# Stacked low-rank decay products, and the gates' 24 columns as four column groups in single precision

## The chip, the cores and the metric

The kernel runs on one core of a Trainium2 chip. The metric is device microseconds of one execution. TensorE is called PE here; VectorE, ScalarE, GpSimd and SyncE are DVE, ACT, POOL and SP in rows of the profile. SP does no arithmetic here: it issues transfers, in order.

## What is computed

One layer of a streaming encoder on 1152 rows of 1024 values: a prompt of 1024 frames and eight running streams of 16 frames. The part that the change touches, cut from the reference:

```python
h = _rmsnorm(x, norm1)
gq, gk, gv, gr, glr, mq, mk, mv, mo, mi, mf = _split_proj(h @ w_in)
log_a = log_sigmoid(glr @ w_gla_a + b_gla_a) / 16     # glr: 16 columns; w_gla_a: 16 x 256
i_pre = mi + b_m_i                                    # 4 columns
log_f = log_sigmoid(mf + b_m_f)                       # 4 columns
# GLA:   S_new = exp(b_last) * S + k_dec^T v,  o = (q * exp(b)) S + scores v,   S = 0 for the prompt
# mLSTM: C_new = decay * C + (ws k)^T v,       num = qk v + w_inter * (q C),    C = 0 for the prompt
x = x + concat(o_A, o_B) @ w_out
x = x + conv_ffn(_rmsnorm(x, norm2))
```

So the projection has 24 narrow columns (mf, mi, glr: "the gates"), and the decay product multiplies the 16 low-rank columns by a 16 x 256 matrix.

## The kernel before

All large products are made in fp32r with both operands split into a high and a low half: `mm3` (lines 93 to 95) issues high x high, high x low and low x high into one accumulation. A weight piece is 128 x 1024; SP loads it into one of two `raw` slots, ACT copies it (high half, line 821), POOL subtracts (low half, line 749). Pieces live in six units in the order `W_ORDER`.

The work of the front part is one list, `front_order`, that every engine walks in this order, each doing its own share of an item, with semaphores between the engines. Rows are in three row blocks (rb) of 384. Items:
- `("turn", rb, half)`: PE transposes the scaled rows (line 957), ACT copies to the high half (837), DVE makes the low half (1160). Blocks 1 and 2 are turned in halves of four.
- `("gate", 0, rb)`: one unit of 24 products, 128 weight columns (24 of them used: mf at 0, mi at 32, glr at 64). DVE takes it from its bank by three or four instructions (lines 1170 to 1174), the low-rank rows into `glr`.
- `("t", t, rb)`: a unit of 24 products for tile t of gq, gk, mq, mk; DVE copies it out (1363), SP stores it.
- `("z", j, rb)`: decay product, 16 x 128 weights by 16 x 384, in single precision (1120); DVE adds the bias (1367).
- `("logs",)`: log-sigmoid of the decays and of the forget gate. DVE line 1179 and 1181, then ACT three Exp (904) and three Ln (908).
- `("n", g, r)`: 128 rows of gv, gr, mo or mv, 24 products of 512 columns; k runs over four weight pieces, two k for each.
- `("w", i)`: ACT and POOL split piece i. From piece 6 on the rule below puts it ahead of the unit after the last use of the piece six earlier, and on ACT it stands at that place of the list, behind whatever is listed ahead of it:

```python
where[i] = min(max(n if shared else n + 1, where[i - 2] + 3, where[i - 1]), len(units))
```

PSUM banks of the front form a ring of four; a unit waits until the entry four before it has been taken. PE does the wait for a unit's weights (`piece_split`) and, for a tile, for all low halves of its row block (`lo_done`).

With that, the order of the kernel before is: gate 0, t0, t1 of block 0; half a turn; t2; half a turn; t3, gate 1; half a turn; t0 of block 1; half a turn; t1 to t3 of block 1; gate 2; t0 of block 2; six z; logs; t1 to t3 of block 2; nine rows of gv (g = 0, weight pieces 5 to 8); and so on with gr, mo, mv and the recurrence of the GLA in blocks of 128 frames (`outputs`, lines 1079 to 1103).

The back part walks `back_order` in the same way: products with w_out (`a` for the GLA half, `b` for the mLSTM half), transposes (`turn_a`, `turn_b` line 1818, `turn_n` line 1826) and the mLSTM (`numbers`, lines 1782 to 1789, `updates`, line 1806). Step 0 is the sample streams, whose states `C_s` SP loads at line 1539; steps 1 to 8 are the prompt. ACT line 1690 is `scaled`, which scales a row of x for `turn_n` when POOL's root (1625) is there. After it the feed-forward part runs to the end; it isn't touched.

Of the kernel before, what the change touches and what calls it, by code (L numbers as in the profile page):

```python
# [12 lines left out]
P = 128  # L13
# [188 lines left out]
def front_memory(nc):  # L202
    return Memory(nc, "p", [
        ("arena", [P, ARENA], F32), ("masks", [P, N_MASKS], F32), ("sig", [P, 512], F32), ("n_out", [P, 2, 512], F32),
        ("w_decay", [RANK, 2 * P], F32), ("gap", [P, 472], F32), ("t_out", [P, 4, RBW], F32), ("ss", [P, RT], F32), ("rstd", [P, RT], F32),
        ("rstd_h", [P, RT, H], F32), ("h1T_hi", [P, KD, ROWS], F32R), ("h1T_lo", [P, KD, ROWS], F32R)])
# [32 lines left out]
def scaled_memory(nc):  # L239
    return Memory(nc, "n", [("gap", [P, 19968], F32), ("rows", [P, JR, D], F32)])  # L240

# [43 lines left out]
def build(nc, a, o):  # L285
    with ExitStack() as top:
# [11 lines left out]
        mem_p, mem_m, mem_f, mem_n = front_memory(nc), back_memory(nc), ffn_memory(nc), scaled_memory(nc)  # L298
# [4 lines left out]
        done = front(nc, a, o, mem_p, mem_m, early, const, cols, col_m, col_d, ssq, power, w, raw, pb, bank, sem, block)  # L303
# [33 lines left out]
W_ORDER = ([PC_GATE] + [PC_T + t for t in range(4)] + [PC_N + 4 * g + q for g in (0, 2, 3, 1) for q in range(4)]  # L337
# [8 lines left out]
def front_order():  # L346
# [50 lines left out]
def pieces_of(x):  # L397
    if x[0] == "gate":
        return [0]
# [34 lines left out]
def front_entries(order):  # L434
    second = False
    out = []
    for x in order:
        second = second or x[:2] == ("n", 1)
        if x[0] in ("gate", "z", "cols", "flip"):
# [13 lines left out]
def front(nc, a, o, mem, mem_m, early, const, cols, col_m, col_d, ssq, power, w, raw, pb, bank, sem, block):  # L453
# [9 lines left out]
    wa = mem["w_decay"]  # L463
    ss, rstd, rstd_h = mem["ss"], mem["rstd"], mem["rstd_h"]

    def carve(at, *shapes):
        for shape in shapes:
# [4 lines left out]
            if len(shape) > 2:  # L472
# [9 lines left out]
    gu, z = (gu0, gu1, gu2), (z0, z1)  # L482
    ones_row, dg = gu0[0:H, 0:P], gu1[0:H, 0:(NC + NB) * H]
    m_ext, lf_ext, g_f, keep, glr = carve(RT * D, [H, EXT], [H, EXT], [H, ROWS], [H, ROWS], [RANK, ROWS])
# [19 lines left out]
             "level_step og_scaled root_step head_roots scored kdn_ready o_squared")  # L504
# [26 lines left out]
    def wait_taken(eng, name):  # L531
        owner, n = ring.taken(name)
        eng.wait_ge(taken[owner], n)

# [72 lines left out]
    def _(sp):  # L607
# [25 lines left out]
        sp.dma_start(const[:, :], a["ident"]).then_inc(g["const_loaded"], 16)  # L633
# [4 lines left out]
        for x in order:  # L638
# [4 lines left out]
            elif x == ("turn", 2, 1):  # L643
                sp.dma_start(wa[:, :], a["w_decay"]).then_inc(g["small_loaded"], 16)
# [55 lines left out]
            elif x[0] == "late":  # L700

                Done.attention_rows(sp)
# [3 lines left out]
                sp.dma_start(mem_m["og_b"][:, 0, :], a["pN"][2, M_STEPS[2]]).then_inc(early.og_in[2], 16)  # L706
                sp.dma_start(mem_m["og_b"][:, 1, :], a["pN"][2, M_STEPS[3]]).then_inc(early.og_in[3], 16)
# [27 lines left out]
    def _(pool):  # L735
        pool.memset(power[:, :], -0.5).then_inc(g["powered"], 1)

# [9 lines left out]
        def lo(i):  # L747
            pool.wait_ge(g["piece_hi"], i + 1)
            pool.tensor_tensor(w_lo[:, i % NS_, :], raw[:, i % 2, :], w_hi[:, i % NS_, :].bitcast(F32),  # L749
# [66 lines left out]
    def _(act):  # L816
        def hi(i):
            act.wait_ge(raw_loaded[i % 2], 16 * (i // 2 + 1))
            if i >= NS_:
                wait_unit_free(act, i - NS_)  # L820
            act.activation(w_hi[:, i % NS_, :], raw[:, i % 2, :], ACT.Copy).then_inc(g["piece_hi"], 1)  # L821
# [9 lines left out]
        def turn_hi(rb, half):  # L831
            if rb == 0:
                act.wait_ge(g["const_loaded"], 32)
# [55 lines left out]

        for x in order:  # L890
            name = x[0]
            if name == "sums":
                sums(x[1])
            elif name == "w":
# [1509 lines left out]
```

## Time and profile before

| | us |
|---|---|
| median of 3 runs | 1441.16 |
| lowest and highest | 1440.81, 1441.31 |
| the profiled execution, its own time | 1443.35 |
| its span, first to last instruction | 1441.6 |

The front part takes the first 438 us, the back part runs to 604 us, the feed-forward part to the end. A matmul's busy time in the rows includes its passage through the array, so matmuls overlap: what one costs in a row of equals is the distance from start to start. A product in single precision appears as two instructions (two passes). Rows of the timeline merge equals; "x12" is their count, and square brackets give the idle time before them and what ended it.

### The profile page before, as it was taken

The page shows a single profiled execution, that of the slowest core. Times are in us where ns is not written, and L with a number is a line of the kernel's source. Part 1 is how long each engine was busy: PE and PEld are TensorE (multiplying, and loading weights), DVE is VectorE, ACT ScalarE, POOL GpSimd, SP SyncE. Part 2 cuts the span into 40 slices and gives each one's busy share as a digit, 9 for nine tenths or more (in the row PEclk, how much of TensorE's full clock was granted, in tenths as well). Part 3 has the DMA queues.
Part 4 walks back from the last instruction along what each step waited for, and adds up shares of the span by engine and source line. Part 5 has one row for each costly group of instructions (what it writes and reads, how often), then busy time and mean ns, then how long its engine had stood idle before and what let it go on. Part 6 is the DMA issues. An engine that isn't in the chain of part 4 may idle for free.

```text
span 1441.6 us, 22554 instructions
## 1 busy us (share of the span) xinstructions
PE 1417.3 (98%) x8769; PEld 1294.9 (90%) x8769; DVE 602.3 (42%) x1233; ACT 416.8 (29%) x881; POOL 467.4 (32%) x447
## 2 busy tenths in 40 slices
PE   7999999999998999999999999999999999999997
PEld 7988888889997788898989999999999999999895
DVE  4453132466733455554243434333333333343436
ACT  6231232244322145741212222121212131303123
POOL 5221333367633244342232323231313131313210
PEclk9999999999999999999999999999999999999998
DMA  6222533334348463121010101010101011111003
GB/s 252 68 79 106 180 113 106 124 111 147 118 160 276 141 213 103 37 80 59 30 59 29 58 29 58 29 58 29 58 18 62 22 50 37 44 40 47 15 21 131
DMA packets 69409, 122.56 MB, mean 85 GB/s; under 512 B 5575, under 2 KB 41155, under 8 KB 68831
## 3 DMA queue, kind: packets, MB, share of 16 engines
q1 hardware_dynamic: 69343, 121.65, 25.4%
q8 instruction: 45, 0.74, 0.2%
q14 instruction: 21, 0.17, 0.0%
HBM read 92.99 MB, written 28.64 MB: 84 GB/s over the span
## 4 chain that ended last, share of the span: by engine, by line
PE 96%; DMA 1%; DVE 1%; SPq 1%; ACT 0%; issue 0%; POOL 0%; ACTq 0%; DVEq 0%
PE bank L93 29%; PE bank L95 29%; PE bank L94 29%; PE bank L1806 1%; PE bank L1030 1%; DMA m_C_sample<-in_s_mc 1%; PE bank L957 1%; PE bank L1087 1%; DVE m_x L2290 1%; PE bank L1103 1%; PE bank L1760 0%; PE bank L1818 0%; PE bank L1789 0%; PE bank L1788 0%; PE bank L1091 0%; DVE m_x L2271 0%
## 5 line engine op out<-in xcount | busy, mean ns | idle before, releaser
L93 PE MATMUL bank<-f_h2T_hi,w_hi 128*128 128x384 f32 x1056 | 354.2, 335 | 0.0
L95 PE MATMUL bank<-f_h2T_hi,w_lo 128*128 128x384 f32 x1056 | 354.0, 335 | 0.0
L94 PE MATMUL bank<-f_h2T_lo,w_hi 128*128 128x384 f32 x1056 | 353.5, 335 | 0.0
L2091 POOL TENSOR_TENSOR f_a_lo<-f_gate_conv,f_a_hi 128x384 fp32r<-128x384 f32 x66 | 67.1, 1016 | 574.1 <-ACT f_a_hi L2140 574.1
L93 PEld LDWEIGHTS bank<-f_h2T_hi,w_hi 128*128 128x128 f32 x1056 | 198.3, 188 | 0.8 <-issue 0.4
L94 PEld LDWEIGHTS bank<-f_h2T_lo,w_hi 128*128 128x128 f32 x1056 | 198.2, 188 | 0.4
L95 PEld LDWEIGHTS bank<-f_h2T_hi,w_lo 128*128 128x128 f32 x1056 | 198.2, 188 | 0.0
L2271 DVE TENSOR_TENSOR m_x<-bank,m_x 128x512 f32<-128x512 f32 x198 | 136.8, 691 | 126.1 <-PE bank L95 126.1
L93 PE MATMUL bank<-w_hi,f_a_hi 128*128 128x512 f32 x396 | 154.4, 390 | 0.4 <-DVE m_x L2271 0.2
L95 PE MATMUL bank<-w_hi,f_a_lo 128*128 128x512 f32 x396 | 154.3, 390 | 0.0
L94 PE MATMUL bank<-w_lo,f_a_hi 128*128 128x512 f32 x396 | 154.3, 390 | 0.0
L2251 DVE TENSOR_SCALAR f_gate_conv<-f_gate_prompt,f_taps 128x384 f32<-128x384 f32 (+1 forms) x66 | 35.7, 541 | 271.8 <-ACT f_gate_prompt L2124 179.4
L749 POOL TENSOR_TENSOR w_lo<-w_raw,w_hi 128x1024 fp32r<-128x1024 f32 x34 | 82.2, 2430 | 137.0 <-ACT w_hi L821 137.0
L2124 ACT ACTIVATE f_gate_prompt<-bank 128x384 f32<-128x384 f32 x44 | 21.7, 492 | 331.6 <-PE bank L95 331.6
L93 PE MATMUL bank<-w_hi,p_h1T_hi 128*128 128x512 f32 x288 | 112.9, 392 | 0.0
L95 PE MATMUL bank<-w_hi,p_h1T_lo 128*128 128x512 f32 x288 | 112.2, 390 | 0.0
L94 PE MATMUL bank<-w_lo,p_h1T_hi 128*128 128x512 f32 x288 | 112.1, 389 | 0.0
L93 PE MATMUL bank<-p_h1T_hi,w_hi 128*128 128x384 f32 x312 | 107.5, 344 | 0.1
L94 PE MATMUL bank<-p_h1T_lo,w_hi 128*128 128x384 f32 x312 | 105.4, 338 | 0.0
L95 PE MATMUL bank<-p_h1T_hi,w_lo 128*128 128x384 f32 x312 | 105.2, 337 | 0.0
L2081 POOL TENSOR_TENSOR w_lo<-w_raw,w_hi 128x1024 fp32r<-128x1024 f32 x42 | 100.4, 2391 | 5.0 <-ACT w_hi L2102 5.0
L93 PEld LDWEIGHTS bank<-w_hi,f_a_hi 128*128 128x128 f32 x396 | 74.3, 188 | 16.8 <-DVE m_x L2271 1.1
(233 smaller groups left out, 2124.7 us busy)
## 6 DMA issues: line engine op xcount, KB each, us to landing
w_raw<-in_w SPq DMA_DIRECT2D x82, 512.0 KB, 3.6
f_raw<-in_w SPq DMA_DIRECT2D x21, 512.0 KB, 3.5
scratch_pN<-p_n_out SPq DMA_DIRECT2D x36, 256.0 KB, 2.1
scratch_pT<-p_t_out SPq DMA_DIRECT2D x36, 192.0 KB, 1.9
p_arena<-in_x SPq DMA_DIRECT2D x9, 512.0 KB, 6.1
p_arena<-scratch_pN SPq DMA_DIRECT2D x18, 256.0 KB, 3.6
m_x<-in_x SPq DMA_DIRECT2D x9, 512.0 KB, 7.0
m_t_in<-scratch_pT SPq DMA_DIRECT2D x9, 512.0 KB, 6.7
```

Of the source, the lines that this page charges most:

```text
L93: pe.matmul(out, stat[0], mov[0], start=start, stop=False)
L94: pe.matmul(out, stat[0], mov[1], start=False, stop=False)
L95: return pe.matmul(out, stat[1], mov[0], start=False, stop=stop)
L749: pool.tensor_tensor(w_lo[:, i % NS_, :], raw[:, i % 2, :], w_hi[:, i % NS_, :].bitcast(F32), ALU.subtract).then_inc(g["piece_split"], 1)
L957: part = lambda j, k: pe.transpose(turn_bank(rb, k)[:, j * P:(j + 1) * P], x_rows[:, rb * JR + j, k * P:(k + 1) * P], ident)
L1030: mm = pe.matmul(out[c * HP:(c + 1) * HP, e, j * 2 * P + at:j * 2 * P + at + QP], half(kx, e)[:, n, j * P + c * HP:j * P + (c + 1) * HP], ...
L1087: pe.matmul(dst(2 * j + e), gsc[:, 2 * j + e, :], vs(2 * j + e), start=True, stop=True, skip_group_check=True)
L2081: pool.tensor_tensor(w_lo[:, unit, :], slots[slot], w_hi[:, unit, :].bitcast(F32), ALU.subtract).then_inc(piece_split, 1)
L2091: pool.tensor_tensor(a_lo[q][:, s], gc[:, n % 2, :], a_hi[q][:, s].bitcast(F32), ALU.subtract).then_inc(a_split, 1)
L2124: act.activation(gp[:, 2 + rb * RBW:2 + (rb + 1) * RBW], g[:, 0:RBW], ACT.Copy).then_inc(g_out, 1)
L2251: ins = dve.tensor_scalar(dst, src(2), tap[2], tap[3], ALU.mult, ALU.add)
L2271: dve.tensor_tensor(x, bank[6 + half], x, ALU.add).then_inc(down_added, 1)
```

## The change

- **Gates.** The gate piece moves from first to fifth in `W_ORDER`. ACT copies its 24 used columns, packed into 32 (`gate_w`), into `sig`, in full precision; POOL doesn't split it. `gate` makes 16 single-precision products for a row block: k = 4n + q goes to column group q, that is to partitions 32q to 32q + 31 of the bank, for the high and the low half of the rows. The bank then holds four partial sums.
- **Fold.** ACT and DVE take the bank as high and low half (`gate_hi`, `gate_lo`); `fold` multiplies both by `unfold`, a matrix of ones and zeros that adds the four groups and puts mf, mi and three copies of the low-rank rows where they are wanted. ACT copies the bank to `low_rank`, DVE takes gates and subtracts for the low half.
- **Decay products.** `w_decay` stands three times on the 128 partitions (high, high, low), and z is one fp32r product with 128 rows.
- **places.** DVE builds `unfold` from the identity and the low part of `w_decay`; SP loads `w_decay` three times.
- **Order.** Tiles come first; the three gate units stand together behind the last turn; z comes in two groups of three, with t1 of block 2 between, and logs behind the second.
- The identity is loaded by ACT's queue, and PE's first transposes wait for it alone.
- The first prompt block of the GLA and of the mLSTM leaves out the products with a state that is zero.
- SP loads `C_s` first in the back part; the two `og_b` loads move behind it, one ahead of and one behind the values; the wait for the stored GLA rows moves there too.
- `turn_b` of the last step moves behind `("b", RT - 2, 1)`.

The diff, cut to its core:

```diff
-W_ORDER = ([PC_GATE] + [PC_T + t for t in range(4)] + [PC_N + 4 * g + q for g in (0, 2, 3, 1) for q in range(4)]
+W_ORDER = ([PC_T + t for t in range(4)] + [PC_GATE] + [PC_N + 4 * g + q for g in (0, 2, 3, 1) for q in range(4)]
...
-    order = [("sums", 0), ("w", 0), ("w", 1), ("turn", 0, 0), gate(0), ("w", 2), ("sums", 1), tile(0, 0), tile(1, 0),
-             ("w", 3), ("scale", 1), ("turn", 1, 0), tile(2, 0), ("w", 4), ("turn", 1, 1), ("sums", 2), ("scale", 2), tile(3, 0), gate(1),
-             ("turn", 2, 0), tile(0, 1), ("turn", 2, 1), ("w", 5)]
-    order += [tile(t, 1) for t in range(1, 4)] + [gate(2), tile(0, 2)]
-    order += [("z", j, rb) for j in range(2) for rb in range(RB)] + [("logs",)] + [tile(t, 2) for t in range(1, 4)]
+    order = [("sums", 0), ("w", 0), ("w", 1), ("turn", 0, 0), tile(0, 0), ("w", 2), ("sums", 1), tile(1, 0), tile(2, 0),
+             ("w", 3), ("scale", 1), ("turn", 1, 0), tile(3, 0), ("w", 4), ("turn", 1, 1), ("sums", 2), ("scale", 2),
+             tile(0, 1), tile(1, 1), ("turn", 2, 0), tile(2, 1), ("turn", 2, 1), ("places",), ("w", 5)]
+    order += [gate(rb) for rb in range(RB)] + [tile(3, 1)] + [("fold", rb) for rb in range(RB)] + [tile(0, 2)]
+    order += [("z", 0, rb) for rb in range(RB)] + [tile(1, 2)] + [("z", 1, rb) for rb in range(RB)] + [("logs",)]
+    order += [tile(2, 2), tile(3, 2)]
...
         load_x(0, JR)
-        sp.dma_start(const[:, :], a["ident"]).then_inc(g["const_loaded"], 16)
...
-                sp.dma_start(wa[:, :], a["w_decay"]).then_inc(g["small_loaded"], 16)
+                sp.wait_ge(g["places_zeroed"], 1)
+                for r in LOW:
+                    sp.dma_start(wa[r, :], a["w_decay"]).then_inc(g["small_loaded"], 16)
...
             elif x[0] == "late":
-
-                Done.attention_rows(sp)
                 Done.attention(sp)
                 Done.row_block_stored(sp, M_STEPS[0] // JR)
                 early.load_tiles(sp, a, mem_m, 0)
-                sp.dma_start(mem_m["og_b"][:, 0, :], a["pN"][2, M_STEPS[2]]).then_inc(early.og_in[2], 16)
-                sp.dma_start(mem_m["og_b"][:, 1, :], a["pN"][2, M_STEPS[3]]).then_inc(early.og_in[3], 16)
...
+            if i == G_AT:
+                for dst, src in GATE_COLUMNS:
+                    c = act.activation(gate_w[:, :, dst], gate_piece[:, :, src], ACT.Copy)
+                c.then_inc(g["piece_hi"], 1)
+                return
...
+        act.dma_start(const[:, :], a["ident"]).then_inc(g["ident_loaded"], 16)
...
+        def gate(x, rb):
+
+            out = enter(x)
+            if rb == 0:
+                pe.wait_ge(g["piece_split"], G_AT + 1)
+                pe.wait_ge(g["lo_done"], KD * RB)
+            for n in range(KD // 4):
+                for t in range(2):
+                    for q in range(4):
+                        k = 4 * n + q
+                        mm = pe.matmul(out[q * 32:(q + 1) * 32, 0:RBW], gate_w[:, k, :],
+                                       hT[t][:, k, rb * RBW:(rb + 1) * RBW].bitcast(F32), start=(n, t) == (0, 0),
+                                       stop=(n, t) == (KD // 4 - 1, 1), skip_group_check=True)
+            mm.then_inc(g["filled"], 1)
+
+        def fold(x, rb):
+
+            out = enter(x)
+            if rb == 0:
+                pe.wait_ge(g["parts_ready"], 2)
+            wait_taken(pe, ("gate", 0, rb))
+            s = slice(rb * RBW, (rb + 1) * RBW)
+            pe.matmul(out[:, 0:RBW], unfold[:, :], gate_hi[:, s], start=True, stop=False)
+            pe.matmul(out[:, 0:RBW], unfold[:, :], gate_lo[:, s], start=False, stop=True).then_inc(g["filled"], 1)
...
-                    for e, c in ((0, 0), (1, 1), (0, 1), (1, 0)):
+                    for e, c in ((0, 0), (1, 1), (0, 1), (1, 0)) if s > 1 else ():
...
                 if (j, rb) == (0, 0):
-                    pe.wait_ge(g["small_loaded"], 32)
-                    wait_taken(pe, ("gate", 0, RB - 1))
+                    wait_taken(pe, ("fold", RB - 1))
                 out = enter(x)
-                pe.matmul(out[:, 0:RBW], wa[:, j * P:(j + 1) * P], glr[:, rb * RBW:(rb + 1) * RBW],
+                pe.matmul(out[:, 0:RBW], wa_parts[:, j * P:(j + 1) * P], low_rank[:, rb * RBW:(rb + 1) * RBW],
                           start=True, stop=True).then_inc(g["filled"], 1)
...
-            dve.tensor_copy(glr[:, s], src[64:64 + RANK, 0:RBW]).then_inc(taken["dve"], 1)
+            dve.tensor_tensor(low_rank[32:64, s], src[32:64, 0:RBW], low_rank[32:64, s].bitcast(F32),
+                              ALU.subtract).then_inc(taken["dve"], 1)
...
-        order += [("turn_b", s)] if s == RT - 1 else []
...
-    order += [("b", RT - 2, 1), ("sum", RT - 2, 1), ("ffn", 1), ("turn_n", 1, 0)]
+    order += [("b", RT - 2, 1), ("turn_b", RT - 1), ("sum", RT - 2, 1), ("ffn", 1), ("turn_n", 1, 0)]
...
         done.products(sp)
+        sp.dma_start(C_s[:, :, :, :], a["s_mc"]).then_inc(g["state_in"], 16)
+        done.attention_rows(sp)
+        load_og(2)
         sp.wait_ge(g["ones_set"], 1)
         load_values(0)
-        sp.dma_start(C_s[:, :, :, :], a["s_mc"]).then_inc(g["state_in"], 16)
+        load_og(3)
...
-                    pe.matmul(dst, qs[:, slot, h, :], C_p[:, 0, h, :], start=True, stop=False)
-                    mm = pe.matmul(dst, am[:, slot, h, :], vin[:, slot, h, :], start=False, stop=True)
+                    if s > 1:
+                        pe.matmul(dst, qs[:, slot, h, :], C_p[:, 0, h, :], start=True, stop=False)
+                    mm = pe.matmul(dst, am[:, slot, h, :], vin[:, slot, h, :], start=s == 1, stop=True)
```

## Rows read from the trace of the kernel before

**Rows 1.** The page, part 1: busy us, share of the span, instructions.
```profile
PE 1417.3 (98%) x8769; PEld 1294.9 (90%) x8769; DVE 602.3 (42%) x1233; ACT 416.8 (29%) x881; POOL 467.4 (32%) x447
```

**Rows 2.** PE's waits: waiting line, releaser, us in total, times, longest.
```profile
PE bank L1818 <- POOL m_hidden L1602: 2.5, 1, 2.5
PE bank L1782 <- DMA m_C_sample<-in_s_mc: 2.1, 1, 2.1
```

**Rows 3.** Stretches: length, busy us (count) by engine, granted clock, DMA share, GB/s.
```profile
74.40:79.00 4.60, 4.60 (x16) 4.60 (x16) 4.41 (x4) 2.43 (x3) 0.00 (x0) 0.50 0.00 0
...
454.40:456.30 1.90, 0.00 (x0) 0.00 (x0) 0.64 (x1) 0.00 (x0) 0.00 (x0) 1.00 0.66 195
...
458.10:461.30 3.20, 3.20 (x39) 1.97 (x31) 0.16 (x1) 1.28 (x4) 2.56 (x2) 0.50 1.00 315
...
592.00:594.00 2.00, 1.16 (x6) 0.62 (x4) 1.93 (x5) 1.71 (x11) 0.76 (x2) 1.00 0.81 266
```

**Rows 4.** Stretches, the one of a gate unit, PE alone.
```profile
60.87:65.03 4.16, 4.16 (x26) 1.00 0.15 51
```

**Rows 5.** PE's timeline (start, us, line, tiles, count), second mLSTM step.
```profile
503.12 0.38 PE L1788 MATMUL bank<-m_C_prompt,m_qs 128*128 128x129 f32 x2
...
503.56 0.39 PE L1788 MATMUL bank<-m_C_prompt,m_qs 128*128 128x129 f32 x2
```

**Rows 6.** PE's timeline, mLSTM step of the sample streams.
```profile
456.41 0.46 PE L1782 MATMUL bank<-m_v_in,m_am 128*128 128x129 f32 x2 [2.10 <-DMA m_C_sample<-in_s_mc]
456.80 0.67 PE L1785 MATMUL bank<-m_C_sample,m_qs_masked 128*32 128x129 f32 x16
457.40 0.49 PE L1782 MATMUL bank<-m_v_in,m_am 128*128 128x129 f32 x2
```

**Rows 7.** The chain that ended last, 66 to 96 us: start, us, line.
```profile
69.35 5.07 PE bank L1120 x12
```

**Rows 8.** ScalarE's timeline at the start.
```profile
12.14 3.88 ACT L837 ACTIVATE p_h1T_hi<-bank,cols 128x384 fp32r<-128x384 f32 x8 [0.40 <-PE bank L957]
```

**Rows 9.** VectorE's timeline, first row blocks.
```profile
33.09 2.19 DVE L1160 SCALAR_TENSOR_TENSOR p_h1T_lo<-bank,cols,p_h1T_hi 128x384 fp32r<-128x384 f32 x4 [0.38 <-ACT p_h1T_hi L837]
```

**Rows 10.** PE's timeline, second row block.
```profile
31.95 1.47 PE L957 MATMUL bank<-ident,p_arena 128*128 128x128 f32 x12
33.18 0.42 PE L93 MATMUL bank<-p_h1T_hi,w_hi 128*128 128x384 f32 x1
```

**Rows 11.** VectorE's timeline, gates, decay products and logs.
```profile
65.22 0.60 DVE L1170 TENSOR_SCALAR p_arena<-bank,cols 4x384 f32<-4x384 f32 x1 [3.60 <-PE bank L95]
...
66.60 0.55 DVE L1174 COPY p_arena<-bank 16x384 f32<-16x384 f32 x1
...
74.46 0.62 DVE L1367 TENSOR_SCALAR p_arena<-bank,cols 128x384 f32<-128x384 f32 x1 [0.66 <-PE bank L1120]
...
74.99 2.62 DVE L1179 SCALAR_TENSOR_TENSOR p_arena<-p_arena 128x1152 f32<-128x1152 f32 x2
```

**Rows 12.** ScalarE's timeline behind the logs.
```profile
84.56 1.99 ACT L821 ACTIVATE w_hi<-w_raw 128x1024 fp32r<-128x1024 f32 x2
```

**Rows 13.** GpSimd's timeline behind the logs.
```profile
85.68 4.76 POOL L749 TENSOR_TENSOR w_lo<-w_raw,w_hi 128x1024 fp32r<-128x1024 f32 x2 [16.55 <-ACT w_hi L821]
```

**Rows 14.** PE's timeline, start of gv.
```profile
89.13 0.39 PE L93 MATMUL bank<-w_hi,p_h1T_hi 128*128 128x512 f32 x1
89.36 0.40 PE L94 MATMUL bank<-w_lo,p_h1T_hi 128*128 128x512 f32 x1
```

**Rows 15.** PE's timeline, GLA products against the state.
```profile
287.01 0.45 PE L1091 MATMUL bank<-p_arena 64*64 64x128 f32 x8
```

**Rows 16.** SyncE's queue at the start of the back part.
```profile
444.78 0.44 SPq L1539 DMA_DIRECT2D m_C_sample<-in_s_mc  x1
```

**Rows 17.** ScalarE's timeline, end of the back part.
```profile
597.51 1.14 ACT L1690 ACTIVATE n_rows<-m_x,rstd 128x1024 f32<-128x1024 f32 x1
```

**Rows 18.** GpSimd's timeline, end of the back part.
```profile
596.08 0.55 POOL L1625 TENSOR_TENSOR rstd<-ssn,power 128x1 f32<-128x1 f32 x1
```

More of the change, by code:

```diff
@@ L302, in build @@
         early, late = Early(sem), Late(sem)
-        done = front(nc, a, o, mem_p, mem_m, early, const, cols, col_m, col_d, ssq, power, w, raw, pb, bank, sem, block)
+        done = front(nc, a, o, mem_p, mem_r, mem_m, early, const, cols, col_m, col_d, ssq, power, w, raw, pb, bank, sem, block)
         done = back(nc, a, o, mem_m, mem_n["rows"], halves_n, early, late, done, const[:, :], cols, col_m, col_d, ssq, ssn, rstd2, power,
@@ L438, in front_entries @@
         second = second or x[:2] == ("n", 1)
-        if x[0] in ("gate", "z", "cols", "flip"):
+        if x[0] in ("gate", "fold", "z", "cols", "flip"):
             out.append((x, "dve"))
@@ L450, in front_entries, with front @@
     return out
-def front(nc, a, o, mem, mem_m, early, const, cols, col_m, col_d, ssq, power, w, raw, pb, bank, sem, block):
+def front(nc, a, o, mem, mem_r, mem_m, early, const, cols, col_m, col_d, ssq, power, w, raw, pb, bank, sem, block):
     HP, QP = P // 2, P // 4
@@ L893, in _ @@
                 sums(x[1])
+            elif name == "places":
+                act.wait_ge(g["small_loaded"], 4 * 16)
+                act.activation(wa_parts[:, :], wa[:, :], ACT.Copy).then_inc(g["wa_hi"], 1)
+            elif name == "gate":
+                rb = x[2]
+                act.wait_ge(g["filled"], ring.filled(x))
+                act.activation(gate_hi[:, rb * RBW:(rb + 1) * RBW], ring.bank(x)[:, 0:RBW], ACT.Copy)\
+                   .then_inc(g["gate_hi"], 1)
+            elif name == "fold":
+                rb = x[1]
+                s = slice(rb * RBW, (rb + 1) * RBW)
+                act.wait_ge(g["filled"], ring.filled(x))
+                act.activation(low_rank[:, s], ring.bank(x)[:, 0:RBW], ACT.Copy).then_inc(g["gate_hi"], 1)
             elif name == "w":
@@ L1086, in outputs @@
                     for e in range(2):
[L1087 to L1089 removed]
+                        mm = pe.matmul(dst(2 * j + e), gsc[:, 2 * j + e, :], vs(2 * j + e), start=True, stop=True,
+                                       skip_group_check=True)
+                        if j and s == 1:
+                            mm.then_inc(g["filled"], 1)
+                    for e, c in ((0, 0), (1, 1), (0, 1), (1, 0)) if s > 1 else ():
                         r = slice(c * HP, (c + 1) * HP)
@@ L1111, in _ @@
                 turn(x[1], x[2])
-            elif name in ("gate", "t"):
+            elif name == "t":
                 tile(x, x[2])
+            elif name == "gate":
+                gate(x, x[2])
+            elif name == "fold":
+                fold(x, x[1])
             elif name == "z":
@@ L1356, in _ @@
             elif name == "gate":
+                rb = x[2]
+                s = slice(rb * RBW, (rb + 1) * RBW)
+                dve.wait_ge(g["gate_hi"], rb + 1)
+                dve.tensor_tensor(gate_lo[:, s], ring.bank(x)[:, 0:RBW], gate_hi[:, s].bitcast(F32),
+                                  ALU.subtract).then_inc(taken["dve"], 1)
+            elif name == "places":
+                dve.wait_ge(g["ident_loaded"], 16)
+                chain.link(dve.memset(places, 0.0))
+                for q in range(4):
+                    r = slice(q * 32, (q + 1) * 32)
+                    gates_, rank = ident[r, q * 32:q * 32 + 2 * H], ident[r, q * 32 + 2 * H:q * 32 + 2 * H + RANK]
+                    at = places[r, 0:64].rearrange("p (n m) -> p n m", m=32)
+                    dve.tensor_copy(at[:, :, 0:H], gates_.rearrange("p (n m) -> p n m", m=H))
+                    dve.tensor_copy(at[:, :, H:H + RANK], rank.unsqueeze(1).to_broadcast([32, 2, RANK]))
+                    u = dve.tensor_copy(places[r, LOW[2]], rank)
+                chain.link(u)
+                dve.tensor_copy(unfold[:, :], places).then_inc(g["parts_ready"], 1)
+                dve.wait_ge(g["wa_hi"], 1)
+                dve.tensor_tensor(wa_parts[LOW[2], :], wa[LOW[2], :], wa_parts[LOW[2], :].bitcast(F32),
+                                   ALU.subtract).then_inc(g["parts_ready"], 1)
+            elif name == "fold":
                 gates(x)
```

46 lines of the change are left out of this document (31 added, 15 removed).

## The prediction

> **What bounds the kernel now.** I read the page first: matmuls keep TensorE (PE) busy for 98% of the span [rows 1], so whatever shortens PE's stream shortens the kernel, unless PE then waits. Next the list of PE's waits: besides the start only two matter, 2.5 us for the scaled hidden rows of the last mLSTM step and 2.1 us for the sample states [rows 2]. The granted clock was read by stretches: it is 0.50, the 1.2 GHz level, behind the decay products (74.4 to 79.0 us) and after the wait for the sample states (458.1 to 461.3 us) [rows 3]. So time can be won by less PE work before 90 us, by the two waits, and by the slow stretches. With that in mind the changed order is followed unit by unit, asking at each wait what is late. All times below are of the profiled execution (span 1441.6 us, own time 1443.35 us); the sum is a difference, and I apply it to the median, 1441.16 us, because the profiled execution is 2.2 us above it.
>
> **Gates.** One gate unit, 24 products of 384 columns, holds PE for 4.16 us [rows 4]; three go: -12.5 us. The replacement is 16 single-precision products for each row block, each issued as two passes, 96 passes in all. A pass of 128 columns costs 0.11 us (four passes, of L1788 and L1789, between the starts at 503.12 and 503.56 [rows 5]), so one of 384 costs 0.33 us. Whether four column groups run at once is shown by the sample states, 128x32 products in single precision on four groups: 16 passes, from 456.80 to the next instruction at 457.40, take 0.60 us [rows 6], where one after the other they would take 1.78 us. Four rounds of 0.11 us are 0.44 us, so two changes of mode cost 0.16 us. Four at once: 24 rounds of 0.33 us plus one entry and exit, 8.1 us. By the gross figure of that row (0.15 us a round) it is 10.9 us, serial 32 us. I take 8.1, since the gates run three units in a row: **-4.4 us**.
>
> The Trainium skill (TensorE: Matmul & The Clock Gate, "Part 3: Packing small matmuls") says that a weight load overlaps running matmuls only if its row group differs, and these all use the same 128 rows. By that rule the gates would take the 10.9 us of the gross figure or more, and the sum below would come to 1442.7 us or more instead of 1439.9. The trace does not agree: 16 passes, each with weights of its own, fit into 0.60 us [rows 6].
>
> **Decay products and fold.** The six decay products take 5.07 us [rows 7]; six stacked ones of one pass each at 0.173 us (4.16/24 [rows 4]) take 1.0: -4.0 us. Six fold passes add +1.0. Behind the old products 16 matmul starts fill the 4.6 us at half clock [rows 3], which at 0.173 us are 2.8 us: -1.8, and with the first one, which lies ahead of that stretch, I take **-2.2**. The stacked form uses all 128 rows for half a microsecond at a time, so I expect no fall there.
>
> **Start.** ident goes out on ScalarE's own queue and PE no longer waits for cols. ScalarE waited 0.40 us for transposes before its first copy [rows 8], and behind that its weight copies bind: **-0.4 us** (between 0 and -0.4).
>
> **Four new waits.** The old order has a full tile behind every second half of a transposed block; the new one does not.
> - A: tile(0,1) now follows turn(1,1) directly and needs its low halves. They end at 33.09 + 2.19 = 35.28 [rows 9], while PE, with turn(1,1) from 31.95, was free at 33.18 [rows 10]: **+2.1 us**, formerly hidden by tile(3,0).
> - B: gate(0) follows turn(2,1) and asks for all 24 low halves: the same chain, **+2.1 us**.
> - C: the first decay product waits until VectorE has taken all three folds. One fold is the old taking of a gate bank (L1170 to L1174), 65.22 to 67.15, 1.9 us or slightly less without the split [rows 11]; three make 5.6 us, starting 1.1 us after tile(3,1) ends (its own output copy, and ScalarE's copy of the fold). They end 6.7 us after it, while fold and tile(0,2) cover 1.0 + 4.2 us: **+1.4 us**.
> - D: the largest. Weight pieces 7 and 8 (last two quarters of gv) reuse the units of t1 and t2, so the rule in the order puts their ScalarE copy behind "logs". Before, the log chain began on VectorE at 74.99 [rows 11], ScalarE came to pieces 7 and 8 at 84.56 [rows 12], and GpSimd finished them at 88.06 and 90.44 (two in 4.76 us from 85.68 [rows 13]): 13.1 and 15.5 us after the start of the log chain. PE began gv at 89.13 and needs piece 7 twelve passes of 0.227 us later, at 91.9 [rows 14]: slack 3.8 us. After: let T be the end of tile(3,1). Decay products at T+6.7, tile(1,2) to T+11.4, second products to T+12.0; VectorE takes these three at 0.62 us each [rows 11] only after the copy of tile(1,2), so the log chain starts at T+14.0. Pieces 7 and 8 are ready at T+27.0 and T+29.4. PE has only two tiles left, begins gv at T+20.3 and wants piece 7 at T+23.1: it waits 4.0 us, works 1.4, and waits 1.0 more: **+5.0 us**. Queued behind that wait on PE is all of gv; behind the logs on ScalarE pieces 7, 8 and 9.
>
> T itself: about 64.1 us by the same addition, so gv's first row ends near 95.0 us, against 94.6 before. Gains of 11.0 and costs of 10.6 + 1.0 (fold) leave +0.6: the front's saving is spent in D and its fellows.
>
> **Clock after the waits.** An idle 1.9 us was followed by the low level until 461.3; one just as long or longer at 593 was not [rows 2, 3]. Of A and B (2.1 us each) I count one fall: 3.2 us at half clock (as from 458.1 to 461.3), +1.6. D is twice as long; I count one fall, about 5 us at half clock (as from 74.4 to 79 once dense work ran again), 2.5 less the 1.0 of its second wait that slow work fills: +1.5. Together **+3.1** (bounds 0 and +6).
>
> **Zero state.** The first prompt block of GLA loses two groups of eight 64x64 passes, 0.45 us each [rows 15]: **-0.9**. The mLSTM block loses four pairs of L1788, eight passes of 0.11 us [rows 5]: **-0.9**.
>
> **Sample states.** C_s went out at 444.78 [rows 16], behind two og_b rows, values and gates. Now only tiles(0) and one store lie ahead, some 4.5 us earlier. But values and og now queue behind its 2 MB, and turn_a(2) and num(0) need them; the tiles of step 0 share the engines with it. Wait: between 0 and -2.1; if it is gone, the slow stretch goes too: half of its 3.2 us, -1.6 [rows 3]. I take **-2.4** of 0 to -3.7; +1 is possible if tiles(0) come late.
>
> **turn_b of the last step** moves behind b(7,1), 2.6 us of work, which fills the 2.5 us. What is late next: ScalarE must now do scaled(5), formerly at 597.51 to 598.65 [rows 17], ahead of its copy for turn_b, and scaled(5) waits for GpSimd's root, which ends at 596.63 [rows 18]. It ends then near 597.8, the copy 0.7 and VectorE's half another 0.7 later, and b(8,0) starts near 599.3. Before, it started one half block of transposes (1.2 us [rows 10]) and a short wait behind 598.65, near 600.1: **-0.8** (0 to -2.5).
>
> The remaining edits (zeroed weights, identity blocks, the extra small loads, the gate's column copies) lie on GpSimd, SP, VectorE and ScalarE while PE works on gates and tile(3,1), 12 us in all; the gate halves are taken some 3 us before fold. If that cover failed, fold would start late by the excess.
>
> **Sum:** -0.4 - 4.4 - 4.0 + 1.0 - 2.2 + 2.1 + 2.1 + 1.4 + 5.0 + 3.1 - 0.9 - 0.9 - 2.4 - 0.8 = -1.3 us; 1441.2 - 1.3 = 1439.9 us.
>
> **Rivals.**
> - *Wait D does not appear, or is mostly hidden* (ScalarE reaches pieces 7 and 8 ahead of the logs, or the log chain is faster): without its 5.0 and its 1.5 of clock, 1433.4 us. Against it: in the trace of before both pieces stand right behind the last logarithm [rows 12], as the order says. Chance 0.17.
> - *The waits come, the clock stays up*, as at 593 us: 1436.8 us. Chance 0.16.
> - *Slower: the low clock holds through the gates.* If wait B drops it and 32-column passes do not bring it back, 8.1 us of gates take 16.2; less the 1.6 already counted for one fall that is +6.5: 1446.4 us. It decides once more than 4 us of the gates' work runs at 0.50. For it: the low level held from 458.1 to 461.3 in just such passes. Against: it rose again there before they ended. Chance 0.10.
> - *The groups do not run at once with 384 columns:* 32 us of gates, 1463.8 us; the sample stage speaks against it. Chance 0.03. With the weight loads of each round in the open, priced by the gross 0.15 us a round: +2.8, 1442.7 us. Chance 0.04.
> - My forecast with its own spread (one clock fall more or less, C_s between 0 and -3.6), 1437 to 1443 us: 0.50.
>
> **How the numbers follow.** About 0.2% (2.9 us) is what a measurement of this kernel can tell from no change. Faster by more: all of the first rival, 0.11 of the second, 0.13 of the forecast: 0.41. Slower by more: the clock rival, the serial one, and 0.03 of the forecast: 0.16. The rest, 0.43, is within. The range runs from 1433, which takes in the first rival, to 1445; above it lie most of the slow-gate case and the serial one, below it the case in which D, the falls and the whole C_s wait go at once.
>
> **What would show it.** In the profile after: 32-column single-precision gate passes in 24 rounds, about 2.6 us for each block; PE idle by some 2 us before tile(0,1) and before gate(0), waiting for VectorE's low halves; 1 to 2 us before the first decay product; 4 to 5 us at gv's first row, released by GpSimd's w_lo; gv's first row ending near 95 us or later; a clock of 1.00 through the decay products. The prediction is wrong if gv starts without a wait, if the clock never falls before 100 us, or if the gates take over 12 us.

## The result and the profile after

| | before | after |
|---|---|---|
| median, us | 1441.31 (5 runs, 1440.81 to 1441.97) | 1448.25 (5 runs, 1445.85 to 1451.39) |
| ratio | | 1.0048, interval 1.0036 to 1.0059 |
| profiled execution: time, span | 1443.35, 1441.6 | 1445.85, 1444.1 |
| PE busy | 1417.3 | 1409.4 |

The changed kernel is 7 us slower, where 1.3 us less was forecast with a range that ended at 1445. PE is busy for 7.9 us less, time at the low clock included, and the span is 2.5 us longer, so in this execution the loss is waiting. The list of PE's waits after (waiting line, releaser, us in total, times, longest), to be read against [rows 2], where two stood besides the start:

```profile
PE bank L995 <- DVE p_arena L1218: 9.3, 2, 7.9
PE bank L93 <- POOL w_lo L768: 3.1, 1, 3.1
PE bank L1911 <- DMA m_og_b<-scratch_pN: 3.1, 1, 3.1
PE bank L93 <- DVE p_h1T_lo L1228: 2.0, 1, 2.0
PE bank L1038 <- DVE p_h1T_lo L1228: 2.0, 1, 2.0
PE bank L1919 <- ACT n_rows L1782: 1.6, 1, 1.6
PE bank L1188 <- DVE g_low_rank L1242: 1.3, 1, 1.3
...
PE bank L1071 <- DVE p_arena L1294: 0.9, 1, 0.9
```

From the top: a second wait of 1.4 us at the start; D; og in the sample stage; A; B; `turn_n`; C; the columns of the decays. A to D and `turn_n` were in the prediction; the start, og and the columns were not.

Stretches of the profile after (length, busy us and count by engine, granted clock, DMA share, GB/s): behind A, the gates, from the first decay products to the second, behind D, and the sample stage. They answer to [rows 3, 4, 7]:

```profile
37.50:40.80 3.30, 3.30 (x11) 3.30 (x12) 1.51 (x2) 2.30 (x4) 2.47 (x5) 0.50 0.17 67
56.35:64.20 7.85, 7.85 (x96) 3.60 (x96) 3.06 (x16) 2.34 (x4) 2.38 (x1) 1.00 0.43 136
75.20:79.90 4.70, 4.70 (x27) 4.59 (x28) 2.20 (x4) 0.00 (x0) 2.32 (x1) 1.00 0.12 42
95.60:98.90 3.30, 3.30 (x9) 2.49 (x9) 0.00 (x0) 0.00 (x0) 2.07 (x1) 0.50 0.63 200
446.00:462.00 16.00, 12.73 (x63) 10.01 (x62) 4.51 (x9) 2.98 (x9) 4.08 (x3) 1.00 0.98 329
```

The 96 gate passes take 7.85 us at full clock; the clock no longer falls at the decay products, but it falls behind A and behind D. Timelines of the profile after (start, us, engine, line, operation, tiles, count, idle time before it and what ended it), in order of time: VectorE's last scaling with GpSimd's subtraction beside it, PE at the start (the last eight transposes, the first and the tenth product), the logs and pieces 7 and 8 on ScalarE, PE at D, VectorE and GpSimd ahead of the columns, SP's queue, and PE at og:

```profile
10.04 2.83 DVE L1218 TENSOR_SCALAR p_arena<-p_arena,p_rstd 128x1024 f32<-128x1024 f32 x1 [0.77 <-POOL p_rstd L760]
...
9.97 5.11 POOL L768 TENSOR_TENSOR w_lo<-w_raw,w_hi 128x1024 fp32r<-128x1024 f32 x2
...
12.93 1.97 PE L995 MATMUL bank<-ident,p_arena 128*128 128x128 f32 x8 [1.39 <-DVE p_arena L1218]
14.96 0.66 PE L93 MATMUL bank<-p_h1T_hi,w_hi 128*128 128x384 f32 x1
...
17.54 0.33 PE L93 MATMUL bank<-p_h1T_hi,w_hi 128*128 128x384 f32 x1
...
88.70 3.28 ACT L946 ACTIVATE p_arena<-p_arena 128x1152 f32<-128x1152 f32 x3
91.89 1.98 ACT L845 ACTIVATE w_hi<-w_raw 128x1024 fp32r<-128x1024 f32 x2
...
91.86 0.39 PE L95 MATMUL bank<-w_hi,p_h1T_lo 128*128 128x512 f32 x1
95.39 0.71 PE L93 MATMUL bank<-w_hi,p_h1T_hi 128*128 128x512 f32 x1 [3.14 <-POOL w_lo L768]
...
100.64 4.54 DVE L1256 SCALAR_TENSOR_TENSOR p_arena<-p_arena 128x1152 f32<-128x1152 f32 x2
...
100.30 2.40 POOL L768 TENSOR_TENSOR w_lo<-w_raw,w_hi 128x1024 fp32r<-128x1024 f32 x1 [2.63 <-ACT w_hi L845]
...
446.40 1.39 SPq L1626 DMA_DIRECT2D m_C_sample<-in_s_mc  x1
447.90 0.61 SPq L1623 DMA_DIRECT2D m_og_b<-scratch_pN  x1
...
458.96 0.66 PE L1911 MATMUL bank<-ident,m_og_b 128*128 128x128 f32 x4 [3.08 <-DMA m_og_b<-scratch_pN]
```

The same steps at the start in the kernel before:

```profile
9.93 0.75 DVE L1150 TENSOR_SCALAR p_arena<-p_arena,p_rstd 128x1024 f32<-128x1024 f32 x1 [1.11 <-POOL p_rstd L745]
...
10.54 4.70 POOL L749 TENSOR_TENSOR w_lo<-w_raw,w_hi 128x1024 fp32r<-128x1024 f32 x2 [0.65 <-ACT w_hi L821]
...
13.60 0.66 PE L93 MATMUL bank<-p_h1T_hi,w_hi 128*128 128x384 f32 x1
...
15.54 0.33 PE L93 MATMUL bank<-p_h1T_hi,w_hi 128*128 128x384 f32 x1
```

The same scaling takes 2.08 us more after the change; GpSimd's subtraction had begun 0.07 us before it, where in the kernel before it began 0.61 us behind it. PE's first product starts at 14.96 instead of 13.60, its tenth at 17.54 instead of 15.54: behind the gap the products stand 0.32 us apart until 17.01, as in the stretches at 0.50, though the granted clock on record there is 1.00.

### The profile page after: what moved, and what is told of

Read it like the earlier page. It is cut to its first block, busy times and chain, and to the rows that moved or that the text cites. A ratio compares the mean times of both kernels' runs of the same rounds, so it can differ in the third digit from the quotient of the medians.

```text
span 1444.1 us, 22584 instructions
## 1 busy us (share of the span) xinstructions
PE 1409.4 (98%) x8769; PEld 1284.6 (89%) x8769; DVE 607.4 (42%) x1251; ACT 419.3 (29%) x890; POOL 465.3 (32%) x447
## 4 chain that ended last, share of the span: by engine, by line
PE 92%; DVE 4%; DMA 2%; ACT 1%; issue 0%; SPq 0%; POOL 0%; ACTq 0%; DVEq 0%; POOLq 0%
PE bank L93 28%; PE bank L95 28%; PE bank L94 28%; PE bank L1899 1%; PE bank L1093 1%; DMA m_og_b<-scratch_pN 1%; PE bank L1150 1%; DVE m_x L2383 1%; PE bank L1038 1%; PE bank L1168 1%; PE bank L1852 0%; PE bank L1911 0%; PE bank L1882 0%; DVE m_x L2364 0%; DMA p_arena<-in_x 0%
## 5 line engine op out<-in xcount | busy, mean ns | idle before, releaser
L93 PE MATMUL bank<-p_h1T_hi,w_hi 128*128 128x384 f32 x288 | 99.5, 346 | 2.2 <-DVE p_h1T_lo L1228 2.0
L94 PE MATMUL bank<-p_h1T_lo,w_hi 128*128 128x384 f32 x288 | 97.4, 338 | 0.0
L95 PE MATMUL bank<-p_h1T_hi,w_lo 128*128 128x384 f32 x288 | 97.3, 338 | 0.0
```

The source lines that it names most:

```text
L93: pe.matmul(out, stat[0], mov[0], start=start, stop=False)
L94: pe.matmul(out, stat[0], mov[1], start=False, stop=False)
L95: return pe.matmul(out, stat[1], mov[0], start=False, stop=stop)
```

## The experiments

The theory after this reading: A to D, the start, og and the columns account for what the change loses, and the lower clock comes with these waits. Rivals are named with each run. The `before` of each run ran on the same chip.

**The back part's edits alone.** The kernel before with the change's zero-state, `turn_b` and `C_s` edits, and nothing of the gates, the decay products or the order of the front.

```diff
+                    if s > 1:
+                        pe.matmul(dst, qs[:, slot, h, :], C_p[:, 0, h, :], start=True, stop=False)
...
+        sp.dma_start(C_s[:, :, :, :], a["s_mc"]).then_inc(g["state_in"], 16)
+        done.attention_rows(sp)
+        load_og(2)
```

> The kernel before with only the back edits: the zero states left out, turn_b of the last step later, C_s ahead of the og rows and values. From the difference of the two traces (GLA -1.0, tiles of step 0 -0.35, og wait +3.3, wait for C_s -2.2, slow stretch behind it -1.5, mLSTM -0.9, turn_b -0.95) it should be 3.7 us faster than the kernel before, 1437.6 us, so that the front part alone is 6 to 10 us slower. By the prediction's sum (-5.0) it would be 1436.3 us. Rival: the og wait depends on the front's changed banks; then it is smaller here and the gain larger.

1437.71 us (8 runs, 1436.01 to 1439.21), ratio 0.9973 (0.9963 to 0.9984). The og wait is there without the front's edits:

```profile
PE bank L1819 <- DMA m_og_b<-scratch_pN: 2.7, 1, 2.7
PE bank L1827 <- ACT n_rows L1690: 1.6, 1, 1.6
```

The back edits gain 3.6 to 3.9 us, so the front's edits lose about 11 us (1.0048 less 0.9973, of 1441), or 9 by the 1.0038 of the next run.

**The changed kernel again, on this chip.** No edit.

> The changed kernel once more, unaltered, for a second profile and more runs. Theory: its waits (start 1.4, two waits of 2.0, 1.3 ahead of the decay products, 3.5 at gv, 0.9 at the columns, 3.1 for og) are there in every run, and what differs from run to run is the number of stretches at the low clock behind them, each worth 1.5 to 3.4 us: times between 1444 and 1451 us that follow each run's mean granted clock, about 1.4 us for 0.001. Rival: one of the waits itself differs (a transfer that lands late in some runs); then the time does not follow the clock.

1446.21 us (5 runs, 1444.17 to 1451.85), ratio 1.0038 (1.0019 to 1.0056), with the same list of waits. The mean granted clock of a run and its time go together: 1444.17 us at 0.996, 1447.75 at 0.992, 1451.85 at 0.990.

**First subtraction later.** GpSimd's first weight subtraction waits until VectorE has scaled the rows.

```diff
+            if i == 0:
+                pool.wait_ge(g["scaled"], JR)
```

> The changed kernel, but GpSimd's first weight subtraction waits until VectorE has scaled all three rows of the first block. Theory: the third scaling took 2.83 us instead of 0.75 because GpSimd's subtraction (2.4 us from 9.97) ran beside it. Then the third scaling takes 0.75 us again, PE's first tile starts at 13.2 to 13.7 instead of 14.96 us, and the time falls by about 1.4 us against the changed kernel. Rival: the third row of x or the identity came late on its queue; then the scaling stays long or starts late, and PE's first tile stays near 15 us.

1443.33 us (10 runs, 1441.63 to 1450.77), ratio 1.0017 (1.0006 to 1.0028). VectorE's third scaling and PE's start in this run:

```profile
10.08 0.75 DVE L1220 TENSOR_SCALAR p_arena<-p_arena,p_rstd 128x1024 f32<-128x1024 f32 x1 [0.77 <-POOL p_rstd L760]
...
7.93 4.91 PE L997 MATMUL bank<-ident,p_arena 128*128 128x128 f32 x24 [7.93 <-DVE p_arena L1220]
13.39 0.45 PE L93 MATMUL bank<-p_h1T_hi,w_hi 128*128 128x384 f32 x1 [0.56 <-POOL w_lo L770]
```

The scaling is back at 0.75 us, the transposes run without a gap, and PE starts at 13.39: the collision is the cause at the start. It cost 1.6 us at the first product and 2.5 us at the tenth, which starts at 15.06 here. The medians differ by more, within the spread of the runs. The profiled run was the slowest of the ten, with two stretches at low clock that the profile after does not have (length, busy us and count by engine, granted clock, DMA share, GB/s):

```profile
264.90:271.60 6.70, 6.70 (x38) 5.30 (x35) 3.77 (x15) 2.29 (x2) 1.29 (x2) 0.50 0.00 0
459.50:466.20 6.70, 6.08 (x17) 4.92 (x18) 0.75 (x1) 1.46 (x4) 3.52 (x3) 0.50 0.99 278
```

**Pieces 7 and 8 ahead of the logarithms.** ScalarE splits piece 7 ahead of the logs and piece 8 between the exponentials and the logarithms (a new item of the order, "lns").

```diff
+    out.remove(("w", 7))
+    out.insert(out.index(("logs",)), ("w", 7))
+    out.insert(out.index(("w", 8)) + 1, ("lns",))
```

> The changed kernel, but weight piece 7 stands ahead of the logs and piece 8 between ScalarE's exponentials and logarithms. Theory: PE's wait of 3.5 us in the first row of gv comes only from ScalarE doing the logs first. Then gv starts without a wait, the clock stays at 1.00 there (it cost 1.7 us), and the time falls by about 5 us against the changed kernel; the logarithms end about 1 us later, which may lengthen the 0.9 us wait at the columns. Rival: the pieces wait for their transfers or for GpSimd; then the wait stays.

1442.2 us (10 runs, 1438.66 to 1443.18), ratio 0.9994 (0.9982 to 1.0006). The wait for `w_lo` is gone from the list and so is the fall behind it; the others stay, with the one at the columns at 0.4 us, where a longer one was thought possible. D is confirmed in place and cause. By the ratios 6 to 8 us are gained, where 5 were expected; the spread of the runs allows either.

**Low halves asked for block by block.** tile(0,1) takes its low halves one k at a time, and a gate unit asks only for those of its own row block.

```diff
-                pe.wait_ge(g["lo_done"], KD * RB)
+            pe.wait_ge(g["lo_done"], KD * (rb + 1))
```

> The changed kernel with the same order, but tile(0,1) waits for the low halves one by one, and each gate unit only for its own row block. Theory: the two waits of 2.0 us were of this form alone. Then both go (under 0.5 us left in each), the clock no longer falls at tile(0,1), and the time falls by 4 to 5.6 us against the changed kernel; the spread of the runs shrinks, since falls of the clock behind those two waits cause part of it. Rival: the low halves come no faster than PE uses them and the wait is spread over the tile; then under 2 us is won.

1441.54 us (10 runs, 1436.87 to 1446.2), ratio 1.0000 (0.9986 to 1.0015). Both waits for low halves are gone from the list; D and og stay at 3.2 and 3.1 us. The wait at the columns is gone from the list too. The ten runs still spread over 9 us, with mean clocks of 0.991 to 0.998, so A and B are not what spreads the runs: that part of the theory failed.

**og ahead of the states.** SP's wait for the stored rows and the first og load go ahead of the 2 MB.

```diff
+        done.attention_rows(sp)
+        load_og(2)
         sp.dma_start(C_s[:, :, :, :], a["s_mc"]).then_inc(g["state_in"], 16)
-        done.attention_rows(sp)
-        load_og(2)
```

> The changed kernel, but SP waits for the GLA rows and loads og of step 2 ahead of the 2 MB of sample states. Theory: the 3.1 us that PE waited for og came from its place behind the states. Then turn_a(2) waits under 0.5 us, the first sample product waits at most 1 us for its states or values, and the time falls by 2 to 3 us against the changed kernel. Rival: the transfers ahead of num(0) are bound by their sum, whatever their order; then the wait moves to num(0) and less than 1 us is won.

1445.2 us (6 runs, 1444.14 to 1448.87), ratio 1.0028 (1.0014 to 1.0041). That is 1.0 us below the median of the changed kernel on this chip, 1.5 us by the spans of the profiles: less than the 2 to 3 us expected, and not clear of the noise, since the intervals overlap. The wait for og is gone, and a smaller one stands further on, at num(0):

```profile
PE bank L1874 <- DVE m_x L2064: 1.0, 1, 1.0
```

**A later subtraction ahead of the columns.** GpSimd's subtraction of piece 9 waits for the two decay rows (L1256).

```diff
+            if i == 9:
+                pool.wait_ge(g["decay_ready"], 2)
```

> The changed kernel, with GpSimd's weight subtraction that began at 100.30 us held back until VectorE has written the two decay rows (L1256). Theory: TensorE's wait of 0.9 us for the columns comes from the two engines working at the same time: the decay rows fall from 4.54 us to 2.6 to 2.9 us (2.62 us in the variant where no subtraction stood beside them, 2.89 us in the kernel before), the columns come 1.6 to 1.9 us earlier and the wait of 0.9 us is gone or under 0.2 us. Rival: the decay rows take 4.5 us for another reason (their operands, ScalarE beside them) and the wait is only the lateness of the logarithms; then they stay at 4.3 to 4.6 us and the wait at 0.7 to 1.0 us. The time of one run does not tell 0.9 us from no change; the two rows decide.

One run, 1449.86 us. The timelines of VectorE and GpSimd in it:

```profile
98.34 2.62 DVE L1258 SCALAR_TENSOR_TENSOR p_arena<-p_arena 128x1152 f32<-128x1152 f32 x2
100.88 1.34 DVE L1261 SCALAR_TENSOR_TENSOR p_arena<-p_arena 4x1152 f32<-4x1152 f32 x1
102.25 2.77 DVE L1263 COPY p_arena<-p_arena 4x1024 f32<-4x1024 f32 x1
104.95 2.41 DVE L1264 COPY p_arena<-p_arena 4x128 f32<-4x128 f32 x1
...
101.11 6.17 POOL L770 TENSOR_TENSOR w_lo<-w_raw,w_hi 128x1024 fp32r<-128x1024 f32 x2 [6.19 <-DVE p_arena L1258]
```

And in the list of PE's waits:

```profile
PE bank L1073 <- DVE p_arena L1296: 1.0, 1, 1.0
```

Half the theory held. Alone, the decay rows take 2.62 us, so the 4.54 us was the subtraction beside them. But the wait did not go: the subtraction now meets the next steps of the same chain, and a copy of 4 x 128 takes 2.41 us instead of the 0.21 us that it takes in the changed kernel. From the decay rows to the scan it is 8.86 us there (100.64 to 109.50) and 9.13 here (98.34 to 107.47). The delay moves along the chain; a run without it was not made.

**Column groups one after the other.** The loops of a gate unit turned, so that the passes of one column group stand in a row: eight in each row block, not 24 as the expectation has it.

```diff
+            for q in range(4):
-            for n in range(KD // 4):
-                for t in range(2):
-                    for q in range(4):
+                for n in range(KD // 4):
+                    for t in range(2):
```

> The changed kernel, with the gates' passes in another order: all 24 passes of one column group in a row, then those of the next group, instead of the four groups in turn. Theory: the four groups work at once only because neighbouring instructions belong to different groups; in a row of one group each pass of 0.32 to 0.33 us stands alone, so 96 passes take 31 us instead of 7.85 us, and the kernel 1460 to 1475 us. Rival: the engine works ahead over the queue and the groups overlap in any order; then the gates stay near 8 us and the time near 1446 us.

One run, 1453.83 us. The stretch of its gates:

```profile
54.40:71.60 17.20, 17.18 (x96) 6.62 (x96) 3.08 (x17) 2.34 (x4) 2.34 (x1) 1.00 0.21 65
```

The timeline of PE there:

```profile
54.42 0.80 PE L1038 MATMUL bank<-p_h1T_hi,p_sig 128*32 128x384 f32 x2 [2.01 <-DVE p_h1T_lo L1228]
55.07 0.81 PE L1038 MATMUL bank<-p_h1T_lo,p_sig 128*32 128x384 f32 x2
55.71 0.84 PE L1038 MATMUL bank<-p_h1T_hi,p_sig 128*32 128x384 f32 x4
56.36 0.84 PE L1038 MATMUL bank<-p_h1T_lo,p_sig 128*32 128x384 f32 x4
```

Neither was right: 17.2 us lies between 31 and 8. The first four passes take 0.64 us for two, one after the other; then four fit into the same 0.65 us, as passes of the next group start beside those of the one before. The rows do not name the group, so this is read from their pattern. In this order two groups overlap; all four did only with neighbours in the stream from different groups, as in the change.

**All four repairs.** The first subtraction, the pieces, the low halves and og, together.

> All four edits of e1 to e4 together in the changed kernel. If the causes are separate, the differences add: 1.4 + 5.5 + 5.2 + 2.8 = 15 us less than the changed kernel's profile (+2.5 us against before), that is 12 us faster than the kernel before, about 1429 us, with a smaller spread of runs since fewer waits are left behind which the clock can fall. If one wait only hides another, the gain is smaller: at least 8 us against the changed kernel.

1430.91 us (6 runs, 1429.97 to 1432.22), ratio 0.9925 (0.9912 to 0.9938): faster than both kernels, and 11.6 us below the median of before on this chip, where 12 were expected, so the differences add. What PE still waits for, besides the start:

```profile
PE bank L1926 <- ACT n_rows L1789: 1.6, 1, 1.6
PE bank L1195 <- DVE g_low_rank L1249: 1.3, 1, 1.3
PE bank L1881 <- DMA m_o_in<-scratch_pN: 1.2, 1, 1.2
...
PE bank L1078 <- DVE p_arena L1301: 0.5, 1, 0.5
```

The mean granted clock of the six runs is 0.997 to 0.998, and they spread over 2.3 us, where the ten runs of each single front repair spread over 4.5 to 9.3 (and the six with og first over 4.7). In the profile the granted clock is 1.00 from PE's first product to its last.

**The repairs, and the decay products later.** As above, with z behind t1 and t2 of block 2, and piece 8 instead of 7 ahead of the logs.

```diff
-    order += [...] + [("fold", rb) for rb in range(RB)] + [tile(0, 2)]
-    order += [("z", 0, rb) for rb in range(RB)] + [tile(1, 2)] + [("z", 1, rb) for rb in range(RB)] + [("logs",)]
+    order += [...] + [("fold", rb) for rb in range(RB)] + [tile(0, 2), tile(1, 2)]
+    order += [("z", 0, rb) for rb in range(RB)] + [tile(2, 2)] + [("z", 1, rb) for rb in range(RB)] + [("logs",)]
```

> As the kernel with four repairs, but the decay products stand one tile later (behind t1 and t2 of block 2), so that VectorE has the folds taken before PE wants them, and piece 8 is split ahead of the logs. Theory: the 1.3 us wait ahead of the decay products goes, and the logs, which end 2 to 3 us later, still come about when VectorE is done with gv's first row: 1 us less than with the four repairs. Rival: the wait at the columns grows by as much; then the same time.

1431.13 us (6 runs, 1429.62 to 1432.95), ratio 0.9925 (0.9911 to 0.9938). C is gone; a wait of 1.2 us for low halves stands in its stead and num(0) waits 1.6 us. No gain over the run before it.

## Why the prediction was wrong

Step by step, in the profiled executions (us, minus is gained). The first product of gv's second row stands for the end of the front's steps, at 94.57 us before and 99.84 after:

| step | predicted | measured |
|---|---|---|
| start | -0.4 | **+2.0** (1.4 at the first product, the rest by the tenth) |
| gates (12.5 to 7.9) and fold | -3.4 | -3.6 |
| decay products and the clock behind them | -6.2 | about -5.8 |
| A, B, one fall | +5.8 | 2.25 + 2.25 (each wait of 2.0 with the entry behind it) and a fall (3.4 us at 0.50, half of it lost: 1.7) = +6.2 |
| C | +1.4 | +1.5 |
| D and its fall | +6.5 | 3.3 + 1.7 = +5.0 |
| so far | +3.7 | +5.2 (the rows themselves) |
| columns | 0 | **+0.95** |
| GLA, mLSTM, turn_b | -2.6 | -1.0 - 0.9 - 0.95 = -2.9 |
| sample states | -2.4 | og +3.3, C_s wait -2.2, its fall -1.5, a wait ahead of them -0.35: **-0.8** |
| sum | -1.3 | +2.5 |

**Right:** A, B, C and D were waits at the places and for the releasers that the prediction named, and removing what PE waits for took A and B away in one run and D in another. The gates ran four groups at once with their weight loads (7.85 us for 96 passes, 8.1 forecast), so the rivals of serial groups and of exposed loads fell, and that of gates at half clock too. For `turn_b` the predicted successor, `turn_n` behind `scaled(5)`, is what is late (L1919).

**The start, +2.4 against the step.** It followed the earlier transposes to ScalarE's weight copies and stopped there. ident left SP's queue, so the weights came earlier too; GpSimd began to subtract at 9.97 instead of 10.54, and VectorE's last scaling, which every later transpose needs, ran into it. The Trainium skill (SBUF — State Buffer, "Who interferes with whom") says that VectorE has ports of its own and shares a second pair with GpSimd. A VectorE instruction needs that pair in a 2-port mode, which copies and `tensor_scalar` can enter, or with two inputs in SBUF while GpSimd reads there; whoever issues first holds it for the whole instruction, and the other is blocked. The trace agrees: a scaling of 128 x 1024 takes 2.08 us more beside a subtraction and a copy of 4 x 128 takes 2.20 more, so each is held for most of one subtraction (2.40 us alone) whatever its own size. The prediction asked which wait is late next, and never which two engines would now work at the same time.

**The sample states, +1.6.** The step said that og and the values queue behind the 2 MB and that turn_a(2) and num(0) need them, and then priced only the C_s wait. og(2) was issued at 447.90, behind C_s at 446.40, and PE waited for it until 458.96. The run with og first shows that the order of the two loads is worth little: og's wait of 3.1 us goes, num(0) waits 1.0 instead, and the medians differ by 1.0 us, within the noise. That the transfers share busy engines there (a DMA share of 0.98) is the likely reason, and not tested.

**The columns, +0.95.** Not in the prediction at all. D moved the decay chain on VectorE against GpSimd's subtractions; from the decay rows to the scan it took 7.3 us before (95.42 to 102.74), where one step met a subtraction, and 8.86 after. That a subtraction lengthens it is shown by the run with the later subtraction. But the chain is only part of the delay. From the decay rows to the diagonals that PE's columns need (L1294, before L1225) it is 22.4 us before and 27.1 after. In between VectorE copies rows of gv, and a copy waits until an earlier row has been stored. After the change:

```profile
125.09 0.69 DVE L1476 COPY p_n_out<-bank 128x512 f32<-128x512 f32 x1 [3.56 <-DMA scratch_pN<-p_n_out]
126.97 0.69 DVE L1476 COPY p_n_out<-bank 128x512 f32<-128x512 f32 x1 [1.18 <-DMA scratch_pN<-p_n_out]
127.72 0.21 DVE L1294 TENSOR_TENSOR p_arena<-p_arena,ident 4x32 f32<-4x32 f32 x2
```

And before:

```profile
116.31 1.49 DVE L1386 COPY p_n_out<-bank 128x512 f32<-128x512 f32 x2 [1.54 <-DMA scratch_pN<-p_n_out]
...
117.85 0.21 DVE L1225 TENSOR_TENSOR p_arena<-p_arena,ident 4x32 f32<-4x32 f32 x2
```

These waits grew from 1.5 to 4.7 us, twice as much as the chain did. Before, PE came to the columns at 121.90, almost 4 us behind the diagonals, so by these rows neither delay alone would have shown. With the low halves asked for block by block the chain took 8.16 us, the waits for stores 4.0, and PE did not wait. No run separates the two, and why the stores landed later is open.

**The falls of the clock.** The sum above ends at +2.5 us, but the medians differ by 7 on the first chip and 3.7 on the second. The profiled run of before was 2 us above its median, the one of after the lowest of five. Over 43 runs of the kernel before, a run is 1.2 us longer for each 0.001 that its mean granted clock is lower. Those runs have a mean of 0.9949 and ten runs of the changed kernel 0.9936: 1.6 us of the difference. The two profiled runs stand the other way round, 0.994 before and 0.995 after, another 1.2 us by the same figure; with both the sum is 5.3 us, between the two measured. The prediction priced one fall each behind A or B and D, as that one profile showed them; it gave no term to falls that come in some runs only. With all four repairs, so without A, B, D and og, the profile has none while PE works: its only low stretch is the end, where PE has nothing left to do and which counts in the mean of those runs too (0.9977). Which wait brings which fall is open. Over the profiles, the clock fell behind A in five of seven, behind D in six of seven and behind B in none of seven; the run that removed A and B spread as before. The fall from 264.9 us in the run with the first subtraction later stands behind none of the waits listed, and three other profiles have one between 252 and 272 us while PE is never idle.

The range ended at 1445 because its slower rivals were single large mishaps with small chances. What happened was three small steps of one sign, the start, the sample states and the columns, 5.0 us in all, and the clock. Two sums of the prediction are off by 0.1 us, which changes nothing: C is 6.7 less 5.2, and 24 rounds at the gross figure are 10.8. And its place for the end of gv's first row, near 95 us, leaves out the 3.1 us of low clock that its sum has; with them it is 98.

## What to carry to other kernels

When an edit brings one engine's work forward, lay the timelines of VectorE and GpSimd beside each other and ask which of their instructions now overlap: a 0.75 us step on the critical path can take 2.8 us without any semaphore saying so. Work taken off PE is gained only if the waits that it covered are removed in the same edit: here the same products lost 0.4% with four waits in the open and gained 0.75% with three of them closed and the start and og put right. And for a load that is put first in a queue, price what it pushes back before counting the wait that it removes.

## What the runs showed of the hardware

Column groups of single-precision passes overlap by how they are interleaved: 96 passes of 384 columns took 7.85 us with the four groups in turn, 17.2 us with eight passes of a group in a row; one pass alone takes 0.32 us. Every pass had a weight load of its own in both.

A VectorE step that starts while GpSimd subtracts two 128 x 1024 operands (2.40 us) is held: a scaling of 128 x 1024 took 2.83 us instead of 0.75, a copy of 4 x 1024 2.77 instead of 0.68, a copy of 4 x 128 2.41 instead of 0.21.

A wait of 2.0 us was followed by 3.4 us at the low clock level at one place (37.5 us) and not at another (56.35 us), in the same execution; the second had the gates' single-precision passes behind it. The first place showed it in five of seven profiles, the second in none.
